# 40 instead of 32 tokens worked by fetched rows, the first eight rows in moved beside the late gated blocks

## What is computed

```
v1, i1 = lax.top_k(s1, 16)                       # per token and head, 8 heads
v2, i2 = lax.top_k(s2, 16)
best, pos = lax.top_k(cand, 16)                  # 16 experts per token and head: 128 of 16384
g = jax.nn.softmax(best, axis=-1)
u = expert_u[idx]                                # rows of 1024
act = gelu(einsum('td,thkd->thk', x, u))
w = g * act
out = einsum('thk,thkd->td', w, expert_v[idx])
```

## Time and profile before

| what | value |
|---|---|
| median of 3 runs | 1249.11 us (1248.88 to 1250.55) |
| the profiled execution | 1250.14 us, span 1248.7 us |
| PE busy | 1217.8 us (98%) |
| DVE busy | 1012.4 us (81%) |
| ACT busy | 711.3 us (57%) |
| POOL busy | 226.8 us (18%) |
| DMA | 266.45 MB, mean 213 GB/s |
| granted TensorE clock, mean | 0.996 |

### The profile page before, as it was taken

How to read it: one execution, slowest core, us unless ns; L and a number is a source line. 1 busy time by engine, 2 the same in 40 slices (tenths; PEclk the granted TensorE clock), 3 DMA queues, 4 the chain that set the end, 5 groups by cost and what they waited for, 6 DMA issues and landing times.

```text
span 1248.7 us, 26983 instructions
## 1 busy us (share of the span) xinstructions
PE 1217.8 (98%) x11426; PEld 1028.8 (82%) x11426; DVE 1012.4 (81%) x1584; ACT 711.3 (57%) x1081; POOL 226.8 (18%) x202
## 2 busy tenths in 40 slices
PE   8999999999999999999999999999999999999996
PEld 6546784988744556648999999999999999999996
DVE  5765775899956767677899999899998888879985
ACT  5763333766645344746545568898875555545553
POOL 1322230345500000000113600000002221215320
PEclk9999999999999999999999999999999999999999
DMA  8520006756665422347546666555569999999981
GB/s 341 199 102 1 2 2 229 274 176 220 216 211 215 143 102 99 139 169 271 203 136 238 221 236 220 188 202 200 175 213 355 345 340 343 346 346 360 380 322 56
DMA packets 51353, 266.45 MB, mean 213 GB/s; under 512 B 5136, under 2 KB 5408, under 8 KB 32544
## 3 DMA queue, kind: packets, MB, share of 16 engines
q1 hardware_dynamic: 40192, 226.76, 50.7%
q0 software_dynamic: 10160, 35.96, 7.9%
q10 hardware_dynamic: 880, 1.99, 0.5%
HBM read 262.04 MB, written 2.10 MB: 212 GB/s over the span
## 4 chain that ended last, share of the span: by engine, by line
PE 83%; DVE 7%; ACT 4%; issue 3%; DMA 2%; POOL 0%; ACTq 0%; DVEq 0%; POOLq 0%
PE bank L708 24%; PE bank L714 24%; PE bank L711 24%; PE bank L1371 2%; DMA ring<-in_expert_v 2%; PE bank L788 1%; PE bank L1149 1%; PE bank L1017 1%; PE bank L912 1%; PE bank L805 1%; PE bank L1319 1%; DMA ring<-in_w_up_t 1%; PE bank L859 1%; DVE HT L1609 1%; DVE arena L1503 1%
## 5 line engine op out<-in xcount | busy, mean ns | idle before, releaser
L708 PE MATMUL bank<-arena 128*128 128x256 f16 (+3 forms) x720 | 215.7, 306 | 0.3 <-DVE arena L1495 0.2
L714 PE MATMUL bank<-arena 128*128 128x256 f16 (+3 forms) x720 | 215.7, 306 | 0.0
L711 PE MATMUL bank<-arena 128*128 128x256 f16 (+3 forms) x720 | 215.7, 306 | 0.0
L1503 DVE SCALAR_TENSOR_TENSOR arena<-ring,arena 128x2048 f16<-128x2048 f32 (+1 forms) x59 | 133.8, 2273 | 34.5 <-ACT arena L2560 34.4
L708 PE MATMUL bank<-cst,arena 128*128 128x224 f16 (+2 forms) x544 | 133.4, 254 | 0.4 <-DVE arena L1503 0.4
L2560 ACT ACTIVATE arena<-ring 128x2048 f16<-128x2048 f32 (+1 forms) x59 | 111.2, 1892 | 39.7 <-PE bank L714 28.9
L714 PE MATMUL bank<-cst,arena 128*128 128x224 f16 (+2 forms) x544 | 133.4, 254 | 0.0
L711 PE MATMUL bank<-cst,arena 128*128 128x224 f16 (+2 forms) x544 | 133.4, 254 | 0.0
L2212 DVE SCALAR_TENSOR_TENSOR X<-ring,X 128x2048 f16<-128x2048 f32 x42 | 96.2, 2290 | 19.5 <-ACT X L2963 19.5
L2212 DVE SCALAR_TENSOR_TENSOR ring<-ring 128x2048 f16<-128x2048 f32 x42 | 96.1, 2289 | 19.1 <-ACT ring L2963 19.1
L3019 ACT CAST arena<-arena 128x448 f16<-128x448 f32 x64 | 36.0, 565 | 130.7 <-PE bank L714 130.7
(11 more groups left out here) (381 smaller groups left out, 3547.9 us busy)
## 6 DMA issues: line engine op xcount, KB each, us to landing
ring<-in_expert_u SPq DMA_DIRECT2D x64, 1024.0 KB, 4.8
ring<-in_expert_v SPq DMA_DIRECT2D x64, 1024.0 KB, 7.7
ring<-in_w_in_n SPq DMA_DIRECT2D x24, 1024.0 KB, 4.9
ring<-in_w_up_t SPq DMA_DIRECT2D x22, 1024.0 KB, 5.0
ring<-in_w_down_n SPq DMA_DIRECT2D x11, 1024.0 KB, 4.8
ring<-in_w_out_n SPq DMA_DIRECT2D x8, 1024.0 KB, 4.8
ring<-in_w_query_t SPq DMA_DIRECT2D x8, 1024.0 KB, 4.8
ring<-in_w_in_t SPq DMA_DIRECT2D x3, 1024.0 KB, 6.8
```

The costliest lines, as they stand in the source:

```text
L708: pe.matmul(out_, stat[0], mov[0], start=start, stop=False, skip_group_check=shared)
L711: pe.matmul(out_, stat[0], mov[1], start=False, stop=False, skip_group_check=shared)
L714: return pe.matmul(out_, stat[1], mov[0], start=False, stop=stop, skip_group_check=shared)
L1503: nv.scalar_tensor_tensor(out=lo, in0=ld.slot(i), scalar=W_UP, in1=hi, op0=ALU.mult, op1=ALU.subtract).then_inc(s["split_lo"], 1)
```

## The change

`NG` goes from 32 to 40, so `NT` from 224 to 216 columns and the gate groups from 28 to 27. The 40 tokens are laid out as two groups: 32 tokens four times over the partitions, and 8 tokens sixteen times, each with its own `h_rows` and `row_sums`. There are 40 fetches in and 40 out. The first eight rows in use one buffer (buffer 0) and are done in turns 32, 36, ... 60, at the end of the turn; the other 72 are spread over turns 64 to 126, eight in seven turns, so that every seventh turn has two. `GATES_IN` now leaves out blocks 38, 45, 53 and 60.

```diff
-NG = 32
+NG = 40
 NT = S - NG
-NK = 128 // NG
+ROW_GROUPS = [(8, 32), (0, 8)]
...
-ROWS_IN = [max(0, min(NG, n - 63)) for n in range(128)]
-ROWS_OUT = [max(0, min(NG, n - 95 + (n >= 110))) for n in range(128)]
-ROW_GELU = 95
+ROWS_EARLY = 8
+ROWS = [min(ROWS_EARLY, max(0, (n - 28) // 4)) if n < 64 else ROWS_EARLY + (72 * (n - 63) + 62) // 63 for n in range(128)]
+ROWS_IN = [min(NG, n) for n in ROWS]
+ROWS_OUT = [min(NG, max(0, n - NG)) for n in ROWS]
+ROW_GELU = 91
...
+def row_buffer(n):
+    return 0 if n < ROWS_EARLY else (n - ROWS_EARLY + 1) % 3
...
             for hf in range(2):
-                pe.matmul(ps.tile("fin", 1, hf)[128 - NG:128, :], m.row_sel, m.row_sums[:, hf * 512:(hf + 1) * 512],
-                          start=True, stop=True)
+                for i in range(2):
+                    pe.matmul(ps.tile("fin", 1, hf)[64:128, :], m.row_sel[:, 64 * i:64 * i + 64],
+                              m.row_sums[i][:, hf * 512:(hf + 1) * 512], start=(i == 0), stop=(i == 1))
...
-    nv.tensor_reduce(m.row_sel, ident.rearrange("p (k f) -> p f k", k=NK), AX.X, ALU.add).then_inc(s["row_sel_one"], 1)
+    nv.memset(m.row_sel, 0.0).then_inc(s["row_sel_one"], 1)
     nv.wait_ge(s["row_sel_one"], 1)
+    for i, (_, count) in enumerate(ROW_GROUPS):
+        at = 64 * i + (32 if i == 0 else 24)
+        nv.tensor_reduce(m.row_sel[:, at:at + count], ident.rearrange("p (k f) -> p f k", f=count), AX.X,
+                         ALU.add).then_inc(s["row_sel_one"], 1)
...
+    place_tokens(0)
+    place_tokens(1)
     ng.dma_start(m.fetched[0], k.d["ffn_g"]).then_inc(s["row_gain_landed"], 16)
     choose(0)
     ng.wait_ge(s["slots_named"], 1)
-    for i in range(NK):
...
+    place_rows(0)
     choose(1)
-    ng.wait_ge(s["rows_placed"], 16 * 3 * NK)
+    place_rows(1)
+    ng.wait_ge(s["rows_placed"], 16 * 3 * (128 // 32 + 128 // 8))
...
     for n in range(2 * NG):
         if n == 0:
-            ng.wait_ge(s["h_rows"], 4)
-        if n == 1:
+            ng.wait_ge(s["h_rows"], 8)
+        if n == ROWS_EARLY:
             ng.wait_ge(*ps.full("u", [q for i, q in enumerate(SPLIT) if k.halves(i) == 2][-1]))
-        if n >= 3:
-            ng.wait_ge(s["rows_used"], n - 2)
+        if row_before(n) is not None:
+            ng.wait_ge(s["rows_used"], row_before(n) + 1)
```

More of the change, by code:

```diff
@@ L154 @@
 NCOLS = _o
-ROWS = [("foxo", 64), ("gdno", 64), ("hgo", 64), ("glao", 64), ("alog", 4), ("dtb", 4), ("foxb", 4), ("glab", 128)]
+ROW_CONSTS = [("foxo", 64), ("gdno", 64), ("hgo", 64), ("glao", 64), ("alog", 4), ("dtb", 4), ("foxb", 4), ("glab", 128)]
 ROW_AT = {}
 _o = 0
-for _n, _w in ROWS:
+for _n, _w in ROW_CONSTS:
     ROW_AT[_n] = (_o, _w)
@@ L161, with row_group, row_landed, row_before @@
 NROWS = _o
+def row_group(r):
+    return 0 if r < 32 else 1
+def row_buffer(n):
+    return 0 if n < ROWS_EARLY else (n - ROWS_EARLY + 1) % 3
+def row_landed(n):
+    return 16 * sum(1 for i in range(n + 1) if row_buffer(i) == row_buffer(n))
+def row_before(n):
+    return max((i for i in range(n) if row_buffer(i) == row_buffer(n)), default=None)
 class Sems(dict):
@@ L435, in memory @@
     g = Arena(t, 128 * NT, 32768)
-    m.h_rows = g.take(1024)
+    m.h_rows = [g.take(1024) for _ in range(2)]
     m.row_sums = m.h_rows
@@ L440, in memory @@
     m.row_at = g.take(NG).bitcast(U32)
-    m.row_gate, m.row_dots, m.row_sel = (g.take(NG) for _ in range(3))
+    m.row_gate, m.row_dots = (g.take(NG) for _ in range(2))
+    m.row_sel = m.rows[:, 256:384]
+    early = Arena(t, 12800, 14336)
     a = Arena(t, 16384, 128 * NT)
@@ L445, in memory @@
     m.s2 = [a.take(128) for _ in range(2)]
-    m.top = [a.take(16, 16) for _ in range(2)]
-    m.idx = [a.take(16, 16) for _ in range(2)]
-    m.idf = [a.take(16, 16) for _ in range(2)]
-    m.best = [a.take(8, 16) for _ in range(2)]
-    m.pos = [a.take(8, 16) for _ in range(2)]
+    m.top = [x_.take(16, 16) for x_ in (early, a)]
+    m.idx = [x_.take(16, 16) for x_ in (early, a)]
+    m.idf = [x_.take(16, 16) for x_ in (early, a)]
+    m.best = [x_.take(8, 16) for x_ in (early, a)]
+    m.pos = [x_.take(8, 16) for x_ in (early, a)]
     m.cand = m.qq[:, 0:8, :]
@@ L3260, in choose, with place_tokens, place_rows @@
             ins.then_inc(s["candidates"], 1)
-    for i in range(NK):
-        ng.dma_start(m.h_rows[i * NG:(i + 1) * NG, :], m.xs[3][0:NG, 0, :]).then_inc(s["rows_placed"], 16)
+    def place_tokens(group):
+        first, count = ROW_GROUPS[group]
+        for i in range(128 // count):
+            ng.dma_start(m.h_rows[group][i * count:(i + 1) * count, :],
+                         m.xs[3][first:first + count, 0, :]).then_inc(s["rows_placed"], 16)
+    def place_rows(group):
+        first, count = ROW_GROUPS[group]
+        per = 128 // (128 // count)
+        c0 = 32 * group
+        for i in range(128 // count):
+            rows, at = slice(i * count, (i + 1) * count), slice(i * per, (i + 1) * per)
+            ng.dma_start(m.row_at[rows, c0:c0 + per], m.places[first:first + count, at]).then_inc(s["rows_placed"], 16)
+            ng.dma_start(m.row_gate[rows, c0:c0 + per],
+                         m.slot_gate[0].rearrange("p h k -> p (h k)")[first:first + count, at]
+                         ).then_inc(s["rows_placed"], 16)
+    place_tokens(0)
+    place_tokens(1)
     ng.dma_start(m.fetched[0], k.d["ffn_g"]).then_inc(s["row_gain_landed"], 16)
```

44 lines of the change are left out of this document (22 added, 22 removed).

## The result

| | median | runs | profiled execution | its span | clock |
|---|---|---|---|---|---|
| before | 1248.70 us (1247.71 to 1250.55) | 12 | 1250.14 us | 1248.7 us | 0.996 |
| after | 1252.83 us (1249.98 to 1256.63) | 12 | 1252.73 us | 1251.4 us | 0.993 |

A forecast was written before the change was run, and what follows sets the result against it. TensorE, busy 98% of the span, was taken as the bound. -20.5 - 0.9 + 7.7 + 0.16 + 0.6 + 3.2 + 1.9 + 0.3 = -7.5 us gave 1242.6 profiled, 1241.6 median; range 1234 to 1250.5.

The forecast's parts named there:

- Fewer columns: All 128 blocks: eight columns fewer per matmul make a block 4.44 us, -20.5 us; one gate group less, -0.9 us.
- Blocks 0 to 30: Before the gated blocks: whole gain taken; GpSimd's extra DMA issues and later first fetch cost nothing.
- Eight rows in, gated blocks: Beside the gated blocks: VectorE becomes longer than TensorE and keeps some waits for ScalarE, a loss of 7.7 us.
- The bound of 12 us: Upper bound on the gated blocks' loss, if all of VectorE's waits there are left.
- Rival B: Gated blocks: VectorE's head start covers the early rows, loss 1 us instead of 7.7, 1234.9 us; chance 0.15.
- The start of the blocks out: Block 64 keeps its time, +0.16 us; VectorE's wait for turn 64's two rows adds 0.6 us (0 to 3).
- 72 rows in 63 turns: Blocks out: VectorE needs 4.13 of 4.44 us and holds; 371 GB/s let pass, landings 1 to 2 us longer.
- rival D: Blocks out: fetch latency over three buffers paces VectorE, deciding from a 10.1 us landing; 1257.6 us, chance 0.08.
- Rival C: Blocks out: the DMA engines' rate binds, 4.49 us a block at 367 GB/s; 1247.8 us, chance 0.16.
- The burst: Block 104: loads get late sooner and start from a fuller queue; wait 1.05 becomes 4.3 us, +3.2 (0 to 8).
- The end: After the blocks: four f32 matmuls instead of two, +1.9 us, and waiting for VectorE's last row, +0.3 us.

The follow-up runs named there:

- experiment 2: Changed kernel with GpSimd's eight products of tokens and gain made before its second search: 1250.46 us, ratio 1.0019 to before.
- experiment 5: Changed kernel with GpSimd's products before its second search and five buffers for rows fetched beside the blocks out: 1242.46 us.
- the sixth: Changed kernel with products ahead and five buffers, but no early rows, all 80 beside the blocks out: 1239.06 us.
- experiments 3: Changed kernel with five buffers in place of three for rows fetched beside the blocks out: 1246.41 us.
- 11: Changed kernel with four buffers in place of three for rows fetched beside the blocks out: 1246.65 us.
- the ninth kernel: Changed kernel with products ahead, five buffers, four early rows, first group's sums ahead and the burst in seven parts: 1234.15 us.

## Why the prediction was wrong

**Fewer columns: right.** 4.44 us for a block, 4.90 us won in 31 blocks for 4.96.

**Blocks 0 to 30, "That costs nothing": wrong.** I had looked for whom GpSimd's later fetch would hold up, and left out what its products do to VectorE: 4 us at 729 us. Moving them gave 2.0 us back in blocks 31 to 63 (experiment 2). It was the head start that went, so the 31 blocks themselves show nothing.

**Eight rows in, gated blocks: the mechanism right, the size wrong.** TensorE's own work in 32 blocks is 32 x 4.44 + 27 x 0.91 = 166.7 us, so the loss was 12.0 us for 7.7. The runs part it: 6.5 us for the eight rows (experiment 5 against 6), 2.0 for the products, and 3.4 that stay with neither. TensorE's waits from 756 us to block 63 in the sixth:

```profile
PE bank L1392 <- ACT ring L3032: 2.4, 5, 1.0
```

It is again the scaled one-hots that are late, in five places, with no row in their way; that TensorE's shorter blocks leave the other two engines too little time would explain it, but no run tests it. The place was as said: scaled one-hots late, and VectorE's waits kept (8.4 of 9.7 us). The bound of 12 us held, just. Rival B is out. What I didn't see is that the waits were usable: the four rows put just ahead of them cost 0.05 us each, the eight 0.8.

**The start of the blocks out: about right.** Block 64 came 0.3 us later than forecast, block 67 lost 0.3 for 0.6.

**72 rows in 63 turns, "so I let it pass, with landings longer by 1 to 2 us": the step that failed.** The forecast held the rate against the DMA engines, and they were not the bound. It then held the landing against the mean time of a row, 10.1 us, with the median of before, 8.2: "Against: the median". The landings came out as forecast, 9.7 us in the median, and 21 of 72 were over 10.1. By the sum of rival D, 9.7 us still make (9.7 + 1.22 + 0.3)/3 = 3.74 us a row of 3.885, so on the mean it held. It didn't hold in the turns with two rows: there a row was asked for 8.9 us ahead, as the prediction itself says, less than the 9.2 to 10.2 us of landing that it had forecast. All late blocks stand three or four behind such a turn. TensorE's loss there was put at nothing and was 5.2 us outside the burst.

That latency against the number of buffers is the cause, is shown by experiments 3 and 11: 7.7 and 6.8 us less in that stretch with the same bytes and the same work. So rival D came true in its mechanism; its own sum had 16 us.

What made landings longer is in good part GpSimd's issue behind VectorE: up to 1.8 us on each fetch as soon as VectorE has no wait in front of the low half. It was in the trace of before, in 8 fetches of 63. Five of the 13 issued from 1138 to 1190 us, where the median of 8.2 is from, were such, while the median over all blocks out was 7.4. It may feed itself: a late row removes the wait, the next issue is slow, the next row later. That loop is read from the records, and no run took the slow issue away by itself.

**Rival C: out.** At 371 GB/s nothing bound; 389 was kept for 240 us, and 399 for 130 us, with TensorE busy throughout.
The Trainium skill's 358 GB/s ("DMA: Bandwidth & Descriptors", Specifications) is worked out there as half of a memory stack's 716 GB/s, a share for each of two cores. Taken as the limit of this one core, as the prediction took it, it would rule out the ninth kernel's 389: the measurement decides.

**The burst: right in size, wrong as a cause by itself.** 3.9 us for 4.3. Spread in four, while fetches were short of time, it won 0.9 us in the stretch and 1.7 in the median, within the noise; spread in seven, once they weren't, 4.8 us; in the kernel before nothing that the median shows. The parts were also smaller and lay elsewhere in seven than in four, so these two don't part the size of a part from the time that fetches had.

**The end: +1.7 and +1.3 for 1.9 and 0.3.** The four f32 matmuls took 3.62 us for 1.88, as said. The last row was as said: TensorE waited 1.31 us for it, 0.2 more than before, and with the first group's sums ahead of it 1.35 us went. The rest of the +1.3 is a wait that the forecast had not, 1.07 us for the last block's weights, with VectorE late from its fetches: with five buffers it is gone, and 1.25 us with it.

## What to carry to other kernels

Before rows are added to an engine's queue, look up which of its waits stand where, not only their sum: four rows in front of waits cost 0.2 us here, eight in even steps 6.5, and one in turn 30 1.0. Check a chain of fetches for its latency over its buffers in the tightest stretch and not on the mean: here it bound at 366 GB/s, where 389 could pass. That latency has to be taken as it will be when the consumer no longer idles. If a change uses up slack, check first what else lived on it: here the head start over the gates, the quick issues of fetches and, as it seems, the cover of a burst of 1.5 MB.
